# The first 18 modulation columns of a hybrid Hyena / latent-attention backbone, on TensorE instead of VectorE

## The reference, cut to what matters

```python
sh1, sc1, g1, sh2, sc2, g2 = split(silu(c) @ mod_w[i] + mod_b[i], 6)        # 6 x 1024 values; the same for c_ctx
hx = xs * (1.0 + sc1) + sh1;  hc = cs * (1.0 + csc1) + csh1
u = short_conv(h @ w_in + b_in, conv_w, conv_b)                              # w_in: 1024 x 3072
hdn = sin(freq[0] * (feats @ fw1 + fb1));  hdn = sin(freq[1] * (hdn @ fw2 + fb2))   # the filter network
```

## Time and profile before

| | us |
|---|---|
| median of 3 runs | 3632.44 (3627.76 to 3632.90) |
| the profiled execution, its own time | 3626.07 |
| its span | 3624.4 |
| TensorE busy | 3313.2 (91%) |
| VectorE busy | 2181.9 (60%) |
| ScalarE busy | 1314.3 (36%) |
| moved by DMA | 410.13 MB, 113 GB/s on average |

### The profile page before, as it was taken

One profiled execution on the slowest core, in us unless ns is written; L12 is line 12 of the kernel. 1 busy time (PEld: TensorE's weight loads), 2 busy tenths in 40 slices (PEclk: granted clock), 3 DMA queues, 4 the chain that ended last, 5 costly groups with the idle time before them and its releaser, 6 DMA issues.

```text
span 3624.4 us, 47839 instructions
## 1 busy us (share of the span) xinstructions
PE 3313.2 (91%) x18246; PEld 2593.8 (72%) x18246; DVE 2181.9 (60%) x3240; ACT 1314.3 (36%) x2215; POOL 313.7 (9%) x510
## 2 busy tenths in 40 slices
PE   3999988998889899999899889999999979999797
PEld 1888645555577688888688766777767758888685
DVE  7999833434446655545577655555556676665676
ACT  2221343343333533333345533333334353333344
POOL 0111143443400000000000200000000000000000
PEclk9999999999989999999999999999999989999899
DMA  6666777987631322221634420000000223333632
GB/s 226 208 203 198 214 143 135 168 156 155 181 128 59 108 82 91 93 79 65 258 99 141 147 71 8 8 14 7 7 25 31 91 93 108 108 99 105 226 99 87
DMA packets 184985, 410.13 MB, mean 113 GB/s; under 512 B 33279, under 2 KB 60223, under 8 KB 183111
## 3 DMA queue, kind: packets, MB, share of 16 engines
q1 hardware_dynamic: 132584, 270.68, 22.7%
q0 software_dynamic: 51936, 131.27, 15.4%
q10 hardware_dynamic: 288, 5.77, 0.4%
HBM read 262.50 MB, written 81.00 MB: 95 GB/s over the span
## 4 chain that ended last, share of the span: by engine, by line
PE 74%; DVE 13%; DMA 7%; ACT 3%; issue 2%; POOL 2%; SPq 0%; DVEq 0%; ACTq 0%
PE ps L622 19%; PE ps L623 19%; PE ps L624 19%; PE ps L2403 3%; PE ps L2337 2%; PE ps L2375 2%; PE ps L2355 2%; PE ps L692 1%; POOL t2z L1961 1%; DMA t2k<-s 1%; DVE mx L2769 1%; PE ps L2246 1%; PE ps L2255 1%; PE ps L2438 1%; DMA traw<-hidden_scratch 1%
## 5 line engine op out<-in xcount | busy, mean ns | idle before, releaser
L622 PE MATMUL ps<-HB,gsp 128*128 128x512 f32 x1232 | 489.0, 397 | 37.6 <-DVE HB L798 22.0
L623 PE MATMUL ps<-HB,gsp 128*128 128x512 f32 x1232 | 485.5, 394 | 0.0
L624 PE MATMUL ps<-HB,gsp 128*128 128x512 f32 x1232 | 484.0, 393 | 0.0
L1076 DVE TENSOR_TENSOR gsp<-graw,gsp 128x512 fp32r<-128x512 f32 x330 | 226.5, 690 | 262.4 <-ACT gsp L1055 261.7
L1055 ACT ACTIVATE gsp<-graw 128x512 fp32r<-128x512 f32 x330 | 206.7, 628 | 329.9 <-PE ps L624 266.6
L622 PEld LDWEIGHTS ps<-HB,gsp 128*128 128x128 f32 x1232 | 234.7, 190 | 91.0 <-issue 21.5
L622 PE MATMUL ps<-tsp,wdh 128*128 128x512 f32 x616 | 243.6, 395 | 35.9 <-DVE tsp L1333 35.8
L624 PEld LDWEIGHTS ps<-HB,gsp 128*128 128x128 f32 x1232 | 234.5, 190 | 50.0
L623 PEld LDWEIGHTS ps<-HB,gsp 128*128 128x128 f32 x1232 | 234.9, 191 | 46.5 <-issue 1.0
L624 PE MATMUL ps<-tsp,wdh 128*128 128x512 f32 x616 | 241.7, 392 | 0.0
L623 PE MATMUL ps<-tsp,wdh 128*128 128x512 f32 x616 | 241.7, 392 | 0.0
(11 more groups left out here) (263 smaller groups left out, 7621.3 us busy)
## 6 DMA issues: line engine op xcount, KB each, us to landing
graw<-in_w_gu SPq DMA_DIRECT2D x176, 256.0 KB, 2.7
mring<-in_mod_w POOLq DMA_DIRECT2D x78, 512.0 KB, 4.6
hidden_scratch<-R SPq DMA_DIRECT2D x154, 256.0 KB, 2.4
traw<-hidden_scratch SPq DMA_DIRECT2D x154, 256.0 KB, 2.6
t2k<-s POOLq DMA_DIRECT2D x80, 256.0 KB, 7.0
t2z<-s POOLq DMA_DIRECT2D x160, 128.0 KB, 7.9
t2w<-w POOLq DMA_DIRECT2D x160, 128.0 KB, 5.6
wd<-in_w_dx SPq DMA_DIRECT2D x6, 2816.0 KB, 14.3
```

Source lines behind the costliest of these rows:

```text
L622: pe.matmul(o, wh, xh, start=start, stop=False, skip_group_check=onto)
L623: pe.matmul(o, wh, xl, start=False, stop=False, skip_group_check=onto)
L624: return pe.matmul(o, wl, xh, start=False, stop=stop, skip_group_check=onto)
L1076: dve.tensor_tensor(gsp[U % 3][:, 1, :], graw[:, q, W_SLOT[i], :], gsp[U % 3][:, 0, :].bitcast(F32), ALU.subtract).then_inc(w.lo, 1)
```

## The change

The first 18 columns are no longer made by VectorE. Their weights are loaded in natural layout (input rows on partitions, 2304 output columns) as 8 tiles `w0[:, k, :]` of 128 x 2304 into the place of `Hs0`, with no wait between them. The condition comes a second time in a small layout (`c2t`, 128 x 16), ScalarE makes its SiLU, `c_silu`. TensorE takes two columns of it as the stationary operand (128 x 2) and streams the weights: four pieces of 512 columns go to output partitions 0, 32, 64 and 96 of bank 5, a fifth of 256 columns to bank 7. The sums are accumulated over k. VectorE copies both banks to SBUF, and six small matmuls with the 0/1 matrix `pick` turn the rows into columns of 128 values; VectorE adds the biases. The order of queues changes with it: the filter's inputs are loaded first, `craw` behind `w0`, and its SiLU is made behind `arguments(1)`; the first sine's arguments are reduced by chunks of 512. `s_mu` gets its 36 counts in the x loop at k = 5, so POOL's `mod_load(3)` starts there.

```diff
+        w0 = place("mod_w0", 12, [P, KD, 18 * P])
+        c_raw, c_silu = (der[:].rearrange("p a b c -> p (a b c)")[:, 16 * i:16 * i + 16] for i in range(2))
...
         def _(sp):
-            sp.dma_start(vecs[:], a["vecs"]).then_inc(s_vec, 16)
-            sp.dma_start(modb[:], a["modb"]).then_inc(s_vec, 16)
-            sp.dma_start(craw[:], a["c2"].partition_broadcast(P)).then_inc(s_cond, 16)
             sp.dma_start(fu[0:EMB, :], a["k_feats"]).then_inc(s_fl, 16)
             sp.dma_start(fw1[:], a["fw1"]).then_inc(s_fl, 16)
             sp.dma_start(fw2[:], a["fw2"]).then_inc(s_fl, 16)
-            for m in range(3 * 6):
-                if m >= 6:
-                    sp.wait_ge(s_mu, (m - 5) * 2)
-                sp.dma_start(mring[m % 6][:], a["mod_w"][m]).then_inc(s_wl[m % 6], 16)
+            sp.dma_start(vecs[:], a["vecs"]).then_inc(s_vec, 16)
+            sp.dma_start(modb[:], a["modb"]).then_inc(s_vec, 16)
+            sp.dma_start(c_raw, a["c2t"]).then_inc(s_vec, 16)
+            for k in range(KD):
+                sp.dma_start(w0[:, k, :], a["mod_w0"][k]).then_inc(s_wl[k], 16)
+            sp.dma_start(craw[:], a["c2"].partition_broadcast(P)).then_inc(s_cond, 16)
...
         def _(act):
-            act.wait_ge(s_cond, 16)
-            act.activation(cond[:], craw[:], ACT.Silu).then_inc(s_silu, 1)
-
+            act.wait_ge(s_vec, 48)
+            act.activation(c_silu, c_raw, ACT.Silu).then_inc(s_silu, 1)
...
             arguments(0, 64)
-            act.wait_ge(s_fr, 1)
             for ch in range(NFC):
+                act.wait_ge(s_fr, ch + 1)
                 x = fa[0:64, 512 * ch:512 * ch + 512]
                 act.activation(x, x, ACT.Sin, scale=2 * math.pi).then_inc(s_fs, 1)
             arguments(1, P)
+            act.wait_ge(s_cond, 16)
+            act.activation(cond[:], craw[:], ACT.Silu).then_inc(s_silu, 1)
...
+            def first_modulations(ks):
+                for k in ks:
+                    pe.wait_ge(s_wl[k], 16)
+                    cond_k = c_silu[:, 2 * k:2 * k + 2]
+                    for j in range(4):
+                        pe.matmul(ps[32 * j:32 * j + 2, 5, :], cond_k, w0[:, k, 512 * j:512 * j + 512],
+                                  start=k == 0, stop=k == KD - 1)
+                    mm = pe.matmul(ps[0:2, 7, 0:256], cond_k, w0[:, k, 2048:18 * P], start=k == 0, stop=k == KD - 1)
+                return mm
+
+            pe.wait_ge(s_silu, 1)
+            pe.wait_ge(s_pad, 1)
+            first_modulations(range(2))
             for ch in range(NFC):
                 pe.wait_ge(s_fs, ch + 1)
                 pe.matmul(bank(ch), fw2[:], fa[0:64, 512 * ch:512 * (ch + 1)], start=True, stop=True
                           ).then_inc(s_fp, 1)
+            first_modulations(range(2, KD)).then_inc(s_fp, 1)
+            pe.wait_ge(s_modadd, 2)
+            for q in range(4):
+                pe.matmul(ps[:, 6, 8 * q:8 * q + 8], junk[:, P * q:P * (q + 1)], cols("pick", 0, 8), start=True, stop=True)
+            for q in range(4, 6):
+                mm = pe.matmul(ps[:, 6, 24 + 2 * q:26 + 2 * q], junk[:, P * q:P * (q + 1)], cols("pick", 0, 2), start=True, stop=True)
+            mm.then_inc(s_fp, 1)
...
+            link(dve.memset(bank(5), 0.0))
+            link(dve.memset(bank(7, 256), 0.0))
+            last = dve.memset(macc[:], 0.0)
             last.then_inc(s_pad, 1)
...
-            first_mods(range(6))
-            reduce_arguments(0, 64)
-            first_mods(range(6, 18))
+            def reduce_arguments(layer, rows, n):
+                for ch in range(NPOS // n):
+                    step = (0, NFC)[layer] + ch
+                    dve.wait_ge(s_fa, NFC + NFC if layer else ch + 1)
...
+            dve.wait_ge(s_fp, NFC)
+            reduce_arguments(0, 64, 512)
+            dve.wait_ge(s_fp, 2 * NFC + 1)
+            dve.tensor_copy(junk[:, 0:512], bank(5)).then_inc(s_modadd, 1)
+            dve.tensor_copy(junk[:, 512:768], bank(7, 256)).then_inc(s_modadd, 1)
+            dve.wait_ge(s_fp, 2 * NFC + 2)
+            four = lambda x, order: x.rearrange(f"p ({order} c) -> p j q c", j=4, q=4)
+            link(dve.tensor_tensor(four(modf[:, 0:32], "j q"), four(ps[:, 6, 0:32], "q j"), four(modb[:, 0:32], "j q"), ALU.add))
+            dve.tensor_tensor(modf[:, 32:36], ps[:, 6, 32:36], modb[:, 32:36], ALU.add).then_inc(s_ms, 3)
...
+                if k == 5:
+                    dve.memset(macc[:], 0.0).then_inc(s_mu, 36)
+            dve.wait_ge(s_silu, 2)
+            reduce_arguments(1, P, NPOS)
```

More of the change, by code:

```diff
@@ L54 @@
 for _name, _n in (("ln_g", 32), ("ln_b", 32), ("b_in", 24), ("conv_w", 72), ("conv_b", 24), ("fbias", 16),
-                  ("b_out", 8), ("gq", 3), ("gkv", 2), ("freq", 2), ("fb", 2)):
+                  ("b_out", 8), ("gq", 3), ("gkv", 2), ("freq", 2), ("fb", 2), ("pick", 8)):
     VEC[_name] = _at
@@ L471, in build @@
             norms[idx, c].adds = (made, split, res)
-        RAW0 = [[48] * 4, [48] * 2 + [0] * 2]
+        RAW0 = [[16] * 4, [16] * 4]
         GC_LOADS = [len(range(i, NP, 3)) for i in range(3)]
@@ L1833, in _ @@
             sp.wait_ge(s_xlo, KD)
-            sp.wait_ge(s_fr, 2)
+            sp.wait_ge(s_fr, NFC + 1)
             sp.dma_start(nt[:, 0:NBX + NBC], a["k_nt"]).then_inc(s_cc, 16)
@@ L2047, in bias @@
                 if first:
-                    act.wait_ge(s_fr, 2)
+                    act.wait_ge(s_fr, NFC + 1)
                     for ch in range(3 * j, 3 + 2 * j):
@@ L2512, in _ @@
                     last = dve.memset(b[:, o:o + 1], 0.0)
+            link(dve.memset(bank(5), 0.0))
+            link(dve.memset(bank(7, 256), 0.0))
+            last = dve.memset(macc[:], 0.0)
             last.then_inc(s_pad, 1)
             modf = modv[:].rearrange("p l m c -> p (l m c)")
-            dve.wait_ge(s_silu, 1)
             def mod_tile(m, slot, loaded, count, conds=(0, 1)):
@@ L2532, in mod_store @@
                                   modb[:, bass.ds(m * 2, 2 * n)], ALU.add).then_inc(s_ms, 1)
-            dve.wait_ge(s_vec, 32)
+            dve.wait_ge(s_vec, 48)
             link(dve.tensor_scalar(turns[:, 0, :], cols("freq", 0, 2), 1.0 / (2 * math.pi), None, ALU.mult))
@@ L2537, in _ @@
                 dve.tensor_copy(bcol[:, m:m + 1], col("b_in", m)).then_inc(s_bc, 1)
[L2538 to L2554, removed]
@@ L2556, in _ @@
-            first_mods(range(6))
-            reduce_arguments(0, 64)
-            first_mods(range(6, 18))
+            def reduce_arguments(layer, rows, n):
+                for ch in range(NPOS // n):
+                    step = (0, NFC)[layer] + ch
+                    dve.wait_ge(s_fa, NFC + NFC if layer else ch + 1)
+                    x, u = fa[0:rows, n * ch:n * ch + n], fu[0:rows, n * ch:n * ch + n]
+                    dve.tensor_scalar(u, x, MAGIC, None, ALU.add).then_inc(s_fc, 1)
+                    dve.wait_ge(s_fc, 3 * step + 1)
+                    dve.tensor_scalar(u, u, -MAGIC, None, ALU.add).then_inc(s_fc, 1)
+                    dve.wait_ge(s_fc, 3 * step + 2)
+                    dve.tensor_tensor(x, x, u, ALU.subtract).then_inc(s_fc, 1)
+                    dve.wait_ge(s_fc, 3 * step + 3)
+                    dve.tensor_scalar(x, x, TURN_MAX, -TURN_MAX, ALU.min, ALU.max).then_inc(s_fr, 1)
@@ L2559, in _ @@
+            dve.tensor_tensor(modf[:, 32:36], ps[:, 6, 32:36], modb[:, 32:36], ALU.add).then_inc(s_ms, 3)
             dve.wait_ge(s_ms, 3)
             dve.tensor_scalar(onep[:, 0:8, :], modv[:, 0, 8:16, :], 1.0, None, ALU.add).then_inc(s_modadd, 1)
-            dve.wait_ge(s_modadd, 1)
+            dve.wait_ge(s_modadd, 3)
             stream_dve_begin(dve, p_in)
@@ L2574, in _ @@
                                       ALU.subtract).then_inc(s_xlo, 1)
-            reduce_arguments(1, P)
+                if k == 5:
+                    dve.memset(macc[:], 0.0).then_inc(s_mu, 36)
+            dve.wait_ge(s_silu, 2)
+            reduce_arguments(1, P, NPOS)
             def mods(i, j, first, after):
@@ L2844 @@
         "b_out": percol(x["hy_b_out"]), "gq": percol(x["mla_gq"]), "gkv": percol(x["mla_gkv"]),
+        "pick": np.array([[float(p == 32 * (i // 2) + i % 2) for i in range(8)] for p in range(P)], np.float32),
         "freq": dup64(x["hy_freq"][0]).T, "fb": np.stack([dup64(x["hy_fb1"][0]), dup64(x["hy_fb2"][0])], 1),
@@ L2856 @@
         "c2": np.stack([x["c"][0], x["c_ctx"]], 0),
+        "c2t": np.stack([x["c"][0], x["c_ctx"]], 1).reshape(KD, P, 2).transpose(1, 0, 2).reshape(P, 2 * KD),
+        "mod_w0": x["mod_w"][0][:, 0:18 * P].reshape(KD, P, 18 * P),
         "x_t": x_all.reshape(KD, P, T_ALL).transpose(1, 0, 2),
```

## The result

| us | before | after |
|---|---|---|
| median | 3630.1 (3623.9 to 3632.9, 4 runs) | 3579.3 (3569.1 to 3584.8, 4 runs) |
| the profiled execution, its own time | 3626.07 | 3569.07 |
| mark (first modulated x tile) | 69.91 | 43.56 |
| first matmul of the stream | 74.01 | 47.66 |

The ratio is 0.9883, interval [0.9858, 0.9907]: 51 us less (50.8), where 21 were forecast. The changed kernel is faster, as expected, but by more than the range allowed (3601 at its low end).

A forecast was written before the change was run, and what follows sets the result against it. The prelude was taken as bound by VectorE's 44 us together with the queue's place of `w_in`; the mark moving from 69.9 to 48.7 gave 21.2 us, so 3632.4 becomes 3611, range 3601 to 3626.

The forecast's parts named there:

- VectorE's columns and the queue's place: Prelude: VectorE's 44 us and `w_in`'s place in SP's queue must go together to move the start of the x tiles.
- the four quarters: New matmuls: four pieces on different output partitions run at once, 2.56 us for each k; one after another 7.70.
- POOL's six tiles: Weight loads moved behind the mark: 8 to 10 us needed, 7 us of slack, costed at nothing.
- the step that took the earlier trace's quarters at the full factor: New matmuls: L2337's quarters run four at once at 1.2 GHz, so 2.56 us for each k.
- the estimate of 3.0 us from the Trainium skill: New matmuls: by the skill's 2.38 ratio, each k costs 3.0 us in place of 2.56, mark 3.5 us later.
- The second filter product: TensorE in the prelude: begins at 18.2, never starved, five instructions of 1.71 us, ends at 26.8.
- so I keep the new matmuls at 1.2 GHz too: Prelude: TensorE's clock stays at the lower level; k = 2 to 7 take 15.4 us, ending at 42.1.
- the turning: End of the prelude: drain, copies, 12 small instructions and additions turn rows into columns, 5.2 us; `onep` at 47.3.
- The rival that I gave 0.17: Prelude: transfers bound it if TensorE's clock rises; mark at 43.5 to 45, gain 25 to 26 us, 3606; chance 0.17.
- the two small products: Filter products before the stream: each ran 8.8 us at the lower clock, the argument against a clock rise.
- behind it all waits are between instructions whose order is unchanged, so I let what the mark gains reach the end: Everything behind the mark: the mark's 21.2 us gain reaches the end of the span, unless a transfer is late.
- That row, 25.00 of 25: Busy time by stretch: TensorE busy all the time from 125 us on, so savings elsewhere there are worth nothing.

The follow-up runs named there:

- e5: Kernel before, with SP issuing five x tiles and the first `w_in` tile ahead of the seventh modulation tile: 3607.5 us, ratio 0.9978, mark 61.28.
- e7: Changed kernel with all four pieces of 512 columns written to the same two output partitions: 3599.5 us (single run), mark 56.19.
- e11: Kernel before with 46 tiny unread matmuls (184 instructions) on TensorE ahead of the second filter product: 3605.9 us, ratio 0.9959.
- e15: Kernel before with 368 waits already reached (184 TensorE instructions, no matmul) ahead of the second filter product: 3604.1 us, ratio 0.9957.
- e14: Kernel before with 64 tiny unread matmuls (256 instructions, one whole block) on TensorE ahead of the second filter product: 3621.6 us, ratio 0.9999.
- e13: Changed kernel with 18 tiny unread matmuls (72 instructions) on TensorE ahead of the stream, a shift of 1: 3587.7 us, ratio 0.9911.
- e17: Changed kernel with 144 waits already reached (72 TensorE instructions, no matmul) ahead of the stream: 3589.0 us, ratio to before 0.9910.
- e1: The changed kernel run again, unchanged, against the kernel before: 3581.3 us, ratio 0.9898.
- e18: The changed kernel unchanged, on the chip of e17: 3578.5 us, ratio to before 0.9894; gain less the mark's gain 12.9 us.
- e8: Changed kernel with the first sine's arguments reduced unchunked: 3592.8 us, ratio to before 0.9921; gain less the mark's gain (extra) 0.7 us.
- e6: Changed kernel with the first `w_in` tile loaded right behind the new weights, `craw` and its SiLU later: 3579.7 us, ratio to before 0.9902.
- the eight kernels: Profiled executions of kernels whose TensorE list is shifted by 0, 1 or 256 instructions: convolution stage 593 to 608 us, mean 602.3.
- the eleven: Profiled executions of kernels whose TensorE list is shifted by 184 or 185 instructions: convolution stage 573 to 604 us, mean 586.8.

## Why the prediction was wrong, step by step

**The direction and the order of things were right.** VectorE's columns and the queue's place did have to go together (e5: the queue alone 8.6 of 26.35 us). The first matmul came at 5.63 (forecast 4.5, between 4 and 6), the product of one k took 2.51 at the lower clock (2.56), the four quarters ran at once (e7), `w_in` landed at 41.6 (41 to 42), and nothing waited for POOL's six tiles. Here 2.51 us at that clock agrees with the step that took the earlier trace rows's quarters at the full factor; the estimate of 3.0 us from the Trainium skill (TensorE: Matmul & The Clock Gate, "Measured speedup vs the span model") would have been too high.

**One number that fits is luck.** The second filter product took 8.4 us, from 18.70 to 27.05, where I had 8.6. But I had it never starved and at the lower clock. It ran at the upper clock, 0.43 us for an instruction, up to its last two, and waited for the sines, which came 1.95 us apart (21.14, 23.09, 25.05). The two errors cancel.

**First step that failed: "so I keep the new matmuls at 1.2 GHz too".** TensorE's clock rose within the new products, first at about 17.8 us and, after a fall at 24.6, again at 31.4. k = 2 to 7 took 10.1 us (27.05 to 37.15) in place of 15.4, and the turning, at the upper clock, 3.3 us (37.15 to 40.42) in place of 5.2. `onep` was ready at 40.4, not 47.3, so that it lay ahead of `w_in`, and the mark came at 43.56, not 48.7. The gain at the mark was 26.35 and not 21.2 us. The rival that I gave 0.17, with 43.5 to 45 for the mark, is what happened at the mark. The argument against it, that the two small products never rose, drew on two stretches of 8.8 and 8.9 us with idling on both sides, while here the new products follow the first filter product at once: TensorE had been busy from 5.63 on at the first rise and from 25.05 on at the second. That this is why it rose was not tested.

**Second step that failed, and the larger one: "behind it all waits are between instructions whose order is unchanged, so I let what the mark gains reach the end".** What lay beyond the mark was put at nothing, because TensorE was read as busy all the time from 125 us on. That row, 25.00 of 25, is a stretch of the stream; in the convolution before, TensorE idled 77.2 of 602.5 us, much of it behind DMAs. The order was unchanged, but 46 more matmuls on TensorE moved the rest of its list by 185 instructions within the 256 of a fetched block. The convolution's stage took 573.0 us in place of 602.5 in the two profiled executions. By itself, in the kernel before, such a shift is worth 16 to 17 us (e11, e15), one of a whole block nothing (e14); taken out of the changed kernel it costs 9.4 +- 6.2 (e13, e17 against e1, e18).

**Third: the base.** The median of three runs, 3632.4, and that of the first comparison, 3630.1, lay 12 and 10 us above the 103 later runs of the same kernel (3620.0). One run of this kernel scatters by 7 us (standard deviation). In the 20 profiled executions of all kernels the stream took 343 to 346 us and everything behind the last `t2w` group 2595 to 2604, but the convolution itself 573 to 608.

**The sum.** 26.35 at the mark, 10 of the base, 9 to 17 of the instructions' place (9.4 measured in the changed kernel, 16 to 17 in the kernel before): 45 to 53, measured 51. Against the base of 103 runs the gain is 40.7 (3620.0 less 3579.3; the changed kernel's three medians are 3578.5, 3579.3 and 3581.3): 26.35, and 14 beyond the mark.

**What stays open.** How the place of the instructions in their blocks turns into waits for `t2w`. (The waits of L2337 for `t2z` do not go with it: 18 to 22 us, mean 19.7, in the eight kernels, 16 to 22, mean 19.5, in the eleven.) A fetch of 16 KB takes 0.9 to 2.1 us of DMA time and comes at another moment beside the convolution's loads; that this delays a load is my guess from the packets' records, and no run moved a single fetch alone. Kernels with the same TensorE list still differ by more than I can explain (extra 0.7 in e8, 12.9 in e18), so other shifts, in the timing of the start, act on that stage too, or chance does. And no experiment looked for the best shift: only 0, 1, 92, 184, 185 and 256, which is 0 again, were run. Of these, 185 with the changed start is the fastest; e6's earlier `w_in` on top of it is not measurably better.

## What to carry to other kernels

Price a change by the mark that it moves, but do not price the rest at zero: a stage that hangs on DMA landings just in time, where a late one costs the wait and then slower matmuls, can answer to a shift elsewhere, here even to instructions that do nothing. Read idle time in the stage itself, and not from a stretch ahead of it. Before crediting an edit with more than its mark gives, run the kernel before with as many idle instructions in the same list, and again with a whole block of them. And take the base from more than three runs where a run scatters by 7 us.

## What the runs showed of the hardware that was not expected

- TensorE's instructions come in packets of 16 KB (118 or 119 of them, 1.93 to 1.95 MB), in the convolution one for 253 to 257 executed instructions. Moving the list of the kernel before by 184 made it 16 to 17 us faster (0.9959 and 0.9957); moving it by 256 changed nothing (0.9999).
- Four fp32 matmuls with 2 stationary columns, all 128 rows and 512 streamed columns each, on output partitions 0, 32, 64 and 96, took 0.86 us together at the upper clock, against 3.44 us on one group (e7): a factor of 4.0.
- The clock of TensorE in the prelude rose to its upper level within the new products (17.8), fell at 24.6, after its weight loads had waited 1.28 and 1.66 us for sines, and rose again at 31.4. The granted clock was 0.91, 0.56 and 0.98 in the three stretches shown above.
- Loads from DRAM into SBUF ran at 412 to 428 GB/s over 18 us, where the earlier trace rows had shown 400.
